# Two of three gate branches computed in Strassen's form, with work moved from VectorE to ScalarE and GpSimd

## The reference, cut to what matters

```
cq, ckv, kr, glu, dq, dk, dv, gates = split_cols(h @ w_in)         # gates: 3 * 1024 columns
...
def attend(q, k, v, scale):
    p = jax.nn.softmax(einsum(q, k) * scale)      # 8 heads; context tokens see 256 keys, latent 512
    return einsum(p, v)
def diff_attend(q, k, v, lam, scale):             # 4 heads, two score maps each
    p = p[:, :, 0] - lam * p[:, :, 1]
...
def merge_branches(gates, o_mla, o_conv, o_diff, w_o_mla, w_o_conv, w_o_diff, w_out):
    g = jax.nn.sigmoid(gates).reshape(*gates.shape[:-1], N_BRANCH, D_MODEL)
    y = (g[..., 0, :] * (o_mla @ w_o_mla) + g[..., 1, :] * (o_conv @ w_o_conv)
         + g[..., 2, :] * (o_diff @ w_o_diff))
    return y @ w_out
```

## Time and profile before

| | us |
|---|---|
| median of 3 runs | 1476.87 |
| lowest, highest run | 1475.78, 1478.08 |
| span of the profiled execution | 1474.6 |

### The profile page before, as it was taken

How to read it: one execution, slowest core, us unless ns; L and a number is a source line. 1 busy time by engine, 2 the same in 40 slices (tenths; PEclk the granted TensorE clock), 3 DMA queues, 4 the chain that set the end, 5 groups by cost and what they waited for, 6 DMA issues and landing times.

```text
span 1474.6 us, 19245 instructions
## 1 busy us (share of the span) xinstructions
PE 1391.2 (94%) x7494; PEld 799.9 (54%) x7494; DVE 783.0 (53%) x1738; ACT 366.1 (25%) x795; POOL 175.2 (12%) x118
## 2 busy tenths in 40 slices
PE   6999999999999999989998878999999999999876
PEld 3444444554444445655554437744677885666543
DVE  2579944568887963433132117894753443444322
ACT  4112314432223012222222224141542202100001
POOL 0021521000011210012221210152000110000000
PEclk9999999999999999999999999999999999999999
DMA  9303120144535348199999978232533478999996
GB/s 386 156 36 110 62 101 13 58 143 157 185 112 203 125 194 351 72 349 417 419 418 420 416 272 350 94 114 79 206 116 143 159 300 365 402 419 420 421 420 249
DMA packets 59550, 347.65 MB, mean 236 GB/s; under 512 B 8388, under 2 KB 15172, under 8 KB 28352
## 3 DMA queue, kind: packets, MB, share of 16 engines
q1 hardware_dynamic: 53856, 335.86, 57.5%
q0 software_dynamic: 5024, 8.40, 1.5%
q10 hardware_dynamic: 576, 2.10, 0.4%
HBM read 343.44 MB, written 11.80 MB: 241 GB/s over the span
## 4 chain that ended last, share of the span: by engine, by line
PE 80%; DMA 10%; DVE 4%; SPq 2%; ACT 2%; issue 1%; DVEq 0%; POOLq 0%; ACTq 0%
PE bank L442 75%; DMA arena<-w_up_in 9%; ACT arena L1289 2%; PE bank L788 2%; SPq L2939 1%; DVE arena L1750 1%; PE bank L542 1%; PE bank L1163 1%; SPq L2953 1%; DMA x<-x_in 0%; DMA arena<-y 0%; DVE am L2036 0%; PE bank L1183 0%; SPq L2905 0%; DVE arena L2138 0%
## 5 line engine op out<-in xcount | busy, mean ns | idle before, releaser
L442 PE MATMUL bank<-arena 128*128 128x512 f32 (+12 forms) x5944 | 1227.5, 441 | 23.7 <-DMA arena<-w_up_in 13.1
L442 PEld LDWEIGHTS bank<-arena 128*128 128x128 f32 (+4 forms) x5944 | 661.3, 161 | 503.3 <-issue 385.7
L1289 ACT ACTIVATE arena<-bank 128x512 f32<-128x512 f32 (+5 forms) x423 | 202.3, 499 | 913.5 <-PE bank L442 802.6
L1750 DVE SCALAR_TENSOR_TENSOR arena<-arena,bank 64x256 f32<-64x256 f32 (+2 forms) x121 | 57.8, 479 | 253.1 <-ACT arena L1289 182.1
L1750 DVE SCALAR_TENSOR_TENSOR arena<-arena,early 128x512 f32<-128x512 f32 (+1 forms) x254 | 177.5, 771 | 0.4
L2036 DVE TENSOR_REDUCE am<-bank 128x1 f32<-128x512 f32 (+1 forms) x96 | 55.5, 599 | 129.9 <-PE bank L442 129.8
L2723 POOL TENSOR_TENSOR arena<-arena 128x512 f32<-128x512 f32 (+1 forms) x32 | 37.3, 1168 | 438.4 <-DVE arena L1750 438.4
L1289 ACT ACTIVATE arena<-bank,am 128x512 f32<-128x512 f32 (+1 forms) x96 | 58.6, 613 | 82.0 <-DVE am L2039 81.8
L2762 POOL DMA_INDIRECT y<-arena,routing x33 | 33.0, 999 | 180.2 <-ACT arena L1289 180.2
L788 PEld LDWEIGHTS bank<-con,arena 128*128 128x128 f32 x240 | 29.8, 141 | 35.2 <-issue 22.4
L788 PE MATMUL bank<-con,arena 128*128 128x128 f32 x240 | 38.6, 275 | 4.8 <-DVE arena L2051 4.7
(11 more groups left out here) (226 smaller groups left out, 824.0 us busy)
## 6 DMA issues: line engine op xcount, KB each, us to landing
arena<-w_gate_in SPq DMA_DIRECT2D x60, 1024.0 KB
arena<-w_up_in SPq DMA_DIRECT2D x60, 1024.0 KB
arena<-w_down_in SPq DMA_DIRECT2D x45, 1024.0 KB, 14.9
arena<-mg_in SPq DMA_DIRECT2D x12, 2048.0 KB, 7.8
arena<-adaT_in SPq DMA_DIRECT2D x40, 512.0 KB, 3.7
arena<-adaT_in SPq DMA_DIRECT2D x16, 1024.0 KB, 7.4
arena<-ada_in SPq DMA_DIRECT2D x6, 2048.0 KB, 15.2
arena<-mo_in SPq DMA_DIRECT2D x6, 2048.0 KB, 8.3
```

Source lines behind the costliest of these rows:

```text
L442: return nc.tensor.matmul(out, w, rhs, start=start, stop=stop)
L1289: return nc.scalar.activation(out, in_, fn, **kw)
L1750: return V.scalar_tensor_tensor(out, in0, sc, in1, op0=op0, op1=op1)
```

## The change

In layer 0 the gate products of branches 0 and 1 are made in Strassen's form (Winograd's order). Two gate tiles form a group `(b, g)`; weights are cut into four blocks (two tiles by two halves of the features), `h` into four (two halves of features by context and latent tokens), and the eight block products of four matmuls with 256 columns become seven: q, x, r, 11, 12, y, z, in this order, with `PRODUCTS = 7`. `n` in `merge_range` now counts these smaller steps: five or so in an A unit, 14 in each of D units 0 to 7 (three and a half products). Four sums of `h` and, per group, four sums of weights and two of products are made by GpSimd. ACT copies q and x out of PSUM, DVE adds or subtracts the other five.

Three things move with it, in layer 0 only: the scaling of the probabilities goes from DVE to ACT (`scale_a`, `scale_d`, behind the next unit's exponential); the output copies go to ACT; and a column is issued as two single steps (`column_step`) that stand apart, one ahead of and one behind the merge tiles of a unit, and in D units also ahead of the tiles of products 3 (11) and 5 (y).

```
-                n = [3, 3, 2] * 8 + [4] * 8 + [8] * 8 + [4] * 8
+                n = [5] * 4 + [6, 6, 6, 5, 5] + [5, 4, 4, 4] * 3 + [5, 4, 4] + [4] * 8 + [gate_steps(0, 1) // 8] * 8 + [4] * 8
...
+                def group_step(b, g, i):                      # TensorE
+                    p, k = divmod(i, 4)
...
+                    name, cls, lhs, rhs = (("q", "a", w11, h[:, 0:4, first]), ("x", "a", w21, h_sums[0]), ("r", "d", weight_sum, h_sums[1]),
+                                           ("11", "d", w12, h[:, 4:8, first]), ("12", "d", w11, h[:, 4:8, second]),
+                                           ("y", "d", w21, h_sums[2]), ("z", "d", w22, h_sums[3]))[p]
+                    if k == 0:
+                        begin(cls, (name, l, b, g))
+                        if name in "x r 12 y".split():
+                            pe.wait_ge(sums_ready, pool_sums({"x": "s1", "r": "s2", "12": "s4", "y": "s3"}[name], b, g))
+                    ins = mm(bank_of[(name, l, b, g)][:, 0:256], lhs[:, k, :], rhs[:, k, :], k == 0, k == 3)
...
+                def scale_a(u):                               # ACT, behind exp_a(u + 1)
+                    act.wait_ge(recips_ready, u + 1)
+                    f(P[:, u % 4, 0:AU[u][2]], P[:, u % 4, 0:AU[u][2]], ACT.Copy, scale=am[:, 8 * (u % 8) + 6:8 * (u % 8) + 7]).then_inc(s["probs_ready"], 1)
...
+                        elif what == "product":               # DVE, merge_tiles
+                            if l == 0 and g >= nA and part != 0 and c[1] in (3, 5):
+                                column_step()
+                            group_tile(b, *c)
...
+                    if l == 0:                                # DVE, a D unit
+                        if u + 1 < len(DU):
+                            probs_d(u + 1)
+                        if u + 2 < len(DU):
+                            peak_d(u + 2)
+                        column_step()
+                        if u + 1 < len(DU):
+                            probs_sum(u + 1)
+                        merge_tiles(nA + u, None if u else 1)
+                        column_step()
+                        continue
...
-                    if nA + u in COLUMN_PAIRS[l]:
-                        ada_column(nA + u)
...
+                    while len(column_done[0]) < len(columns[0]):
+                        column_step()
...
+                def sums_ahead(b, g):                         # GpSimd
...
+                    G.tensor_tensor(w21, w21, w22, op=ADD).then_inc(sums_ready, 1)
...
+                    G.tensor_tensor(weight_sum, w11, w21, op=ADD).then_inc(sums_ready, 1)
+                def sums_behind(b, g):
+                    pool.wait_ge(full["a"], A[("q", l, b, g)])
+                    G.tensor_tensor(w11, w12, weight_sum, op=ADD).then_inc(sums_ready, 1)
+                    pool.wait_ge(full["a"], A[("x", l, b, g)])
+                    G.tensor_tensor(w21, weight_sum, w22, op=SUB).then_inc(sums_ready, 1)
...
+                def upper(b, g):
...
+                def corner(b, g):
```

More of the change, by code:

```diff
@@ L255, in attn_units, with merge_at, gate_steps, pool_sums @@
                     [(i, t, seen[t]) for i in range(HD) for t in tiles])
[L259 removed]
+        PRODUCTS = 7
+        GROUPED = ((0, 1), ())
+        N_GROUPS = 4 * len(GROUPED[0])
+        def merge_at(l, r):
+            b = 0
+            while r >= gate_steps(l, b) + 4 * KD:
+                r -= gate_steps(l, b) + 4 * KD
+                b += 1
+            return b, r
+        def gate_steps(l, b):
+            return 16 * PRODUCTS if b in GROUPED[l] else KD * KD
+        def pool_sums(what, b, g):
+            n = 4 * b + g
+            if what == "corner":
+                return 6 * n + (9 if n < N_GROUPS - 1 else 7)
+            if n == 0 and what in ("s1", "s2"):
+                return {"s1": 2, "s2": 3}[what]
+            return 6 * n + {"s1": 1, "s2": 2, "s4": 4, "s3": 5, "u": 6}[what]
         MERGE = (1, 0, 2)
@@ L282, in merge_done @@
             for r_ in range(r0, r1):
-                b, r = divmod(r_, ALL)
-                if r < GATES and r % KD == KD - 1:
-                    done.append(("gate", b, r // KD))
[L286 to L293, removed]
+                b, r = merge_at(l, r_)
+                gates_ = gate_steps(l, b)
+                if b in GROUPED[l]:
+                    if r < gates_ and r % 4 == 3:
+                        done.append(("product", b, divmod(r // 4, PRODUCTS)))
+                    if r >= 4 * PRODUCTS and (r - 3) % (4 * PRODUCTS) == 0 and r < gates_ + 4:
+                        done.append(("gates", b, (r - 3) // (4 * PRODUCTS) - 1))
+                elif r < gates_ and r % KD == KD - 1:
+                    done.append(("gate", b, r // KD))
+                if r >= gates_ and r % 4 == 3:
+                    done.append(("branch", b, (r - gates_) // 4))
             return done
@@ L2716, in _ @@
                 add_channels(cv)
+                if l == 0:
+                    sums_behind(0, 0)
+                    upper(0, 0)
+                    sums_ahead(0, 1)
+                    corner(0, 0)
                 pool.wait_ge(s["conv_sq"], seen(l, "conv_sq", CT))
                 add_channels(lora)
+                if l == 0:
+                    for n in range(1, N_GROUPS):
+                        sums_behind(n // 4, n % 4)
+                        upper(n // 4, n % 4)
+                        if n < N_GROUPS - 1:
+                            sums_ahead((n + 1) // 4, (n + 1) % 4)
+                        corner(n // 4, n % 4)
                 for b, done in ((1, "merge_part"), (2, "yt_ready")):
```

243 lines of the change are left out of this document (204 added, 39 removed).

## The result

| | us |
|---|---|
| before, median of 4 runs beside it | 1477.47 |
| changed, median of 4 runs (1489.79 to 1497.58) | 1492.39 |
| ratio, 95% interval | 1.0109 (1.0081 to 1.0137) |
| span of the profiled executions | 1474.6 and 1492.2 |

What follows compares the result with a forecast made beforehand. TensorE was taken to bound the stage, VectorE close behind. -13.7 - 1.5 + 5.0 (A units) + 1.7 + 7.7 + 0.5 + 2.5 = +2.2 us gave a median of 1479.1 us, range 1468.5 to 1488.

Steps and rivals of the forecast that it cites:

- Gate products: Branches 0 and 1: 224 matmuls of 256 columns replace 128 of 512 at half the time each; gain 13.7 us.
- Output copies: Copies leave VectorE for ScalarE: TensorE's 1.2 us of waits go; with a shorter wait at unit 4, gain 1.5 us.
- Scaling by ScalarE: A units: scaling queues behind the exponential; waits of 2.1 us in four units, 0.4 in the first, 0.5 in unit 9.
- GpSimd beside VectorE: GpSimd's sums and VectorE shut each other out for whole instructions; 2.0 us in A units, 2.6 in odd D units.
- second rival: GpSimd's lock makes VectorE the bound of D units 0 to 7: bank waits 14.0 us, median 1488.4; chance 0.17.
- A to D: At the first D transposes, shorter cover, a column step and later scaling use up the slack; wait of 1.7 us.
- Odd D units: Units 1, 3, 5, 7: product y waits for 11's bank behind column steps, 5.1 us, plus 2.6 from GpSimd; 7.7.
- Second half of the D units: In the later D units the chain is longer by ScalarE's scaling; 0.5 us.
- Tail: Behind the stage, late columns delay the first half's load, so TensorE waits ahead of branch 2's tiles; 2.5 us.
- T + 3.6: T is TensorE's end of the stage; the last column, then the first half's load, was expected 3.6 us behind it.
- nearly each new wait there is paid in full: In the stage from 216 to 466 us, new TensorE waits were carried to the end one to one.
- a stage that ends 8 later: Stated test: the prediction is wrong if the stage ends more than 8 us later than before.

Runs made afterwards that it cites:

- e9: Changed kernel with the edits of e4, e6 and e7 together; 1467.79 us, ratio 0.9936.
- e11: e9 without Strassen's form: gates in 128 matmuls of 512 columns, no GpSimd sums of weights or products; 1479.82 us, ratio 1.0008.
- e8: Changed kernel, GpSimd's sums of weights in branch 1 cut to 8 columns; output not the reference's, total 1524.26 us not used, only the stage read.
- e10: e9 with eight instead of four of D unit 0's merge steps ahead of the first D transposes; 1467.17 us, ratio 0.993.
- e1: Changed kernel, odd D units 1 to 7: no column step ahead of product 11's tile, three together ahead of y's; 1485.8 us, ratio 1.0062.
- e7: Changed kernel, column steps re-placed: three in each of D units 0 to 7, none where a bank waits; 1480.83 us, ratio 1.0023.
- e6: Changed kernel, first half's load after the stage waits for the 27th column's load, not the last column's work; 1486.87 us, ratio 1.0066.
- e5: Kernel before the change, with TensorE made to wait for three ScalarE copies in each of D units 1, 3 and 5; 1495.48 us, ratio 1.0127.
- e2: Changed kernel, idle 256-column matmuls (6, 5, 6) in place of the wait ahead of product y in D units 1, 3, 5; 1489.53 us, ratio 1.0085.
- e4: Changed kernel, VectorE instead of ScalarE scales the probabilities in the A units; 1488.4 us, ratio 1.0075.
- e3: Changed kernel, modulation columns begin in A unit 22 instead of 25, their loads' gates not followed; 1526.78 us, ratio 1.0332.

## Why the prediction was wrong

- **Gate products.** Right. D unit 2, without a wait, takes 7.76 us instead of 8.57, which leaves 0.216 us a pass (0.2155 in the earlier trace rows), and e9 against e11 leaves 9 to 12 us net of their partners.
- **Output copies.** Right: TensorE's waits for them (1.2 us) are gone from its list.
- **Scaling by ScalarE.** Right, unit by unit: behind A units 9, 11, 13, 19, 21 the waits are 0.51, 0.73, 0.30, 1.18, 0.23 (0.5, 0.75, 0.3, 0.75, 0.3 forecast), and one of 0.49 behind unit 23, which was not forecast. In the first unit 0.53 (0.4).
- **GpSimd beside VectorE.** In the A units it can only be part of the 2.5 us that are left by subtraction; in D units at least 3.5 instead of 2.6 (e8). The second rival's 14.0 us of bank waits did not come: they are 8.0.
- **A to D.** 1.67 us; forecast 1.7, and the shorter cover is shown by e10, where four more steps take the wait away. **Odd D units.** 8.0; forecast 7.7, through the chain that was named (e1, e7). That the sum is so close is in part luck: the order alone gives at most 4.5 (e8) instead of 5.1, the sums at least 3.5 instead of 2.6. And the prediction put sums of the next group beside all four units, while behind unit 7 no group follows: it waits 0.39, the other three 2.1 to 2.8.
- **Second half of the D units.** Undersized: twice 1.24 instead of 0.5 in all; a column step ahead of the sum in units with 512 keys, gone in e7.
- **Tail.** Cause right (e6): the first half's load was issued at 483.77, 10.3 us behind the last transposes (473.48), where T + 3.6 would have been 9.2; before, it was 9.1 us ahead of them. Size 3.83 instead of 2.5.
- **The step that failed** is the one that turned waits into time, "nearly each new wait there is paid in full". They were paid more than in full: by the clock. The prediction read the clock of 1.00 in the stage and then left it out of the sum, as if it were a constant; yet 1.00 held there because TensorE hardly waited. Five waits drew 8.6 us of low clock, and each wait a pause of 0.3 that its listed length leaves out, 3.3 us together. The waits themselves were forecast to grow by 15.9 (17.4 less the 1.5 that go) and grew by 18.5 as listed. So from the forecast's +2.2 to the profiled +17.6: 2.6 for waits, mostly the tail and the second half of the D units, 8.6 for the clock, 3.3 for the pauses, 2.5 in short gaps, less the 1.6 that come back. The clock alone decides the range: without its 8.6 us, an estimate from these rows, the median would be 1483.8. By its own test, "a stage that ends 8 later", the prediction is wrong: 13.4 later.

What stays open: the 2.5 us in short gaps, known by subtraction only; and which of the waits of 1.6 to 2.1 us will lower the clock.

## What to carry to other kernels

When a change adds waits to a TensorE that had been at the full clock, price each long one twice: its length, and what the rows show a low stretch to cost (1.7 us here, 2.3 to 2.6 behind some waits of 3.9 us and more). Work that an engine does "meanwhile" belongs behind the instructions that empty a bank, in portions small enough that no unit is overrun; moving it there was worth 11.6 us (e7), about as much as the cheaper products bring. And undo the parts of a mixed change one by one: here the core was worth about 10 us (e9 against e11), and three of its companions together, with the low clock that they drew, cost 25 (e9 against the changed kernel).

## What the runs showed of the hardware

The low clock cost 1.70 to 1.72 us (the missing shares of 2-us windows) in all five places of the changed kernel, and 1.7 behind a wait of 4.77 (e5). The missing shares come to 3.4 us behind waits of 3.91 (e1), 4.99 (e2) and 5.71 (e5), but there the low stretch began 1.6 to 2.2 us before the wait ended, while TensorE was still idle, and 2.3 to 2.6 us of it fell on work. Between 200 and 560 us waits up to 1.63 us never lowered the clock. The 1.66 or 1.67 ahead of the first D transposes did in e2 and not in the changed kernel, e1, e4, e6 and e8. The same wait of 1.70 in the first unit did in the changed kernel, e3 and e6, and did not in e1, e2, e7 and e8, though these kernels are alike up to there. 1.88 (e3) and 1.89 did, 2.12 did not, 2.08 and 2.09 did, and every one of 2.5 and more did. The Trainium skill (TensorE: Matmul & The Clock Gate, Part 1) says that the number of cold matmuls at the start of one and the same kernel varies from run to run; these runs show the like in the middle of a kernel, for whether a given wait lowers the clock at all. Each wait also cost about 0.3 us beside its listed length (D units 1, 3, 5 and 7). Idle matmuls in place of the wait held the clock, at no cost in time, where a free bank could take them (e2).
